# Summing gathered expert rows by 64x64 products on the four quarters of TensorE, one token tile after the other

## The chip, the cores and the metric

One core of one Trainium2 chip runs the whole program. The metric is the device time of one execution in microseconds (us); lower is better. The engines are TensorE (PE in the profile, its weight loads PEld), VectorE (DVE), ScalarE (ACT), GpSimd (POOL) and SyncE (SP). A float32 product is recorded as two MATMULs with a weight load each, so 16 records of a 128x512 product are 8 products.

## The reference

One step of a 2-layer decoder trunk, for 512 prompt tokens and 64 sample tokens. Each layer normalises x, runs three token mixers, merges and projects them back onto x, and then adds the output of a retrieval of single-neuron experts. That last part is where the change is:

```python
def _peer(h, w_query, subkeys, w_up, w_down):
    q = (xt @ w_query).reshape(n, PEER_HEADS, 2, PEER_DKEY // 2)        # 8 heads
    s = jnp.einsum('nhpd,pkd->nhpk', q, subkeys)
    s1, i1 = lax.top_k(s[:, :, 0], PEER_TOPK)                            # top 16
    s2, i2 = lax.top_k(s[:, :, 1], PEER_TOPK)
    cand = (s1[..., :, None] + s2[..., None, :]).reshape(n, PEER_HEADS, 256)
    best, ic = lax.top_k(cand, PEER_TOPK)
    expert = ...                                                         # i1 * 128 + i2
    gate = jax.nn.softmax(best, axis=-1)
    up = jnp.take(w_up, ek, axis=0)                                      # one row of 1024 a choice
    act = jax.nn.gelu(jnp.einsum('nd,nhkd->nhk', xk, up)) * gk
    down = jnp.take(w_down, ek, axis=0)
    return jnp.einsum('nhk,nhkd->nd', act, down)                         # added to x
```

All is float32. Every token has 8 x 16 = 128 choices, each with an up row and a down row of 1024 floats, from tables of 16384 rows.

## The kernel before

The 576 tokens lie in 5 tiles: four of 128 prompt tokens, tile 4 with the 64 sample tokens. The stage with the change is `score_expert_stage`, once in each layer. A **choice** is one gather for one tile: 128 rows (one for each partition) of 2048 floats, the up row and the down row side by side, 1.05 MB. Tile 4 puts two of its choices into one gather, so there are 4 x 128 + 64 = 576 gathers, worked through in 288 **groups** of two.

What a group goes through, engine by engine, each engine in the order in which its program is written:

- POOL (L2826) issues the gather into one of the places of a ring. It waits until the choice that last lay in that place has been summed (`downs_done`).
- DVE (L2868) multiplies the up row with the normalised token and sums the product, one instruction a choice. Between a group's dot products and its weights stands one quarter of the routing of a coming head, if the table `ROUTE_AT` has one for this group: the top-16 searches over scores (`Router.part`, L2404 to L2443), which give the ids that later gathers need.
- ACT (L2933) takes the gelu, DVE (L2880) multiplies it with the gates to `weight`, and ACT (L2944) makes a diagonal matrix of each choice's 128 weights.
- PE (L3036) multiplies the diagonal with the down row: two products of 128x128 by 128x512 a choice, added up in PSUM over all of a tile's choices. After the second the choice's place is free. x itself goes into the same sum by a product with the identity (`add_x`, L3002), so that at a tile's end ACT only copies PSUM back to x (`copy_x`, L2920).
- From the group `GATES_AT` on, one choice of two is not summed by PE: DVE adds weight times down row onto x or onto `own` (`BY_VECTOR`, `add_own`, L2857).

Also inside the stage: queries (L2966, eight products each, in a half of 256 or 128 columns and one of 320) and scores (L2995) for the later heads, which PE makes ahead of the sums of the group named in `asking`, and which ACT copies out (L2892, L2907) after that group's diagonals. Each query's weights (512 KB) come by SP into a ring of three. Tiles 0 and 1 are worked through together, head by head (`TOGETHER = 2`), the others one by one; so a head of routing lasts for 16 groups at first. In layer 0, the groups after `GATES_AT` carry products for the next layer as well (`following.tensor`, L1335 and L1330).

The ring of places (`place_of`): ten places for the first `BEGUN` = 90 choices, eight up to choice `EXTENDED` = 244, then ten again, two of them in room that is free once the last query is done. Before choice `FREE_FIRST` = 3, POOL waits for the end of the output projection.

Of the kernel before, what the change touches and what calls it, by code (L numbers as in the profile page):

```python
# [16 lines left out]
D = 1024  # L17
# [2450 lines left out]
TOGETHER = 2  # L2468
HEADS = [(n, h) for h in range(PH) for n in range(TOGETHER)] + [(n, h) for n in range(TOGETHER, TILES) for h in range(PH)]
BY_GROUP = [(n, h * TOPK + c) for n, h in HEADS[:(TILES - 1) * PH] for c in range(0, TOPK, GROUP)]  # L2470
BY_GROUP += [(TILES - 1, c) for c in range(0, COUNT[TILES - 1], GROUP)]
ROUTE_AT = {}
for _h in range(PH):
    _start = _h * TOGETHER * STEP
    _parts = {0: (1, _h), 8: (0, _h + 1), 12: (TOGETHER, _h)} if _h < PH - 1 else {0: (1, _h), 8: (TOGETHER, _h)}
    for _at, _head in _parts.items():
        ROUTE_AT.update({_start + _at + k: _head + (k,) for k in range(4)})
for _i, _head in enumerate(itertools.product(range(TOGETHER + 1, TILES), range(PH), range(4))):
    ROUTE_AT[TOGETHER * PH * STEP + _i] = _head
# [8 lines left out]
EXTENDED = 244  # L2488
Q_RING = 3
NEAR = 2 * P  # L2490
ASKED = ((0, 2), (3, 4), (6, 9), (11, 13))
FIRST_ASKED, REST_ASKED = ((3, 5), (5, 6), (8, 10), (12, 13)), (0, 2)

FREE_FIRST = 3
BEGIN, BEGUN = (8, 9, 7, 0, 1, 2, 3, 4, 5, 6), 90
# [21 lines left out]
ROUTES_DONE = max(max(ROUTE_AT), TILE_END[TOGETHER] + 5)  # L2517
BATCHES = ((0, 1, 2), ROUTES_DONE + 3), ((3,), TILE_END[TILES - 2] + 5)
# [45 lines left out]
BY_VECTOR = [q for q in range(2 * GATES_AT, PAIRS - 6) if q % 2 == 1]  # L2564
BY_TENSOR = [q for q in range(PAIRS) if q not in BY_VECTOR]
SUMMED = list(itertools.accumulate(0 if q in BY_VECTOR else 1 for q in range(PAIRS)))
TILE_OF = [n for n, c0 in BY_GROUP for k in range(GROUP)]
FIRST_SUM = min(q for q in BY_TENSOR if TILE_OF[q] == LAST_TILE - 1)
FIRST_OWN = min(q for q in BY_VECTOR if TILE_OF[q] == LAST_TILE)
added_by = lambda q: len([k for k in BY_VECTOR if k <= q])  # L2570


class NextNorm:
# [13 lines left out]
    def sync(self, sp):  # L2587
# [17 lines left out]
        else:  # L2605
# [3 lines left out]
            for i in range(2):  # L2609
                sp.wait_ge(s.added, len(BY_VECTOR))  # L2610
                sp.wait_ge(s.downs_done, SUMMED[PAIRS - 5 + 2 * i])
                to, src = self.places.first_slab(i)
                sp.dma_start(to, src).then_inc(s.in_slab[i], 16)

    def scalar(self, act, i):
# [3 lines left out]
        for n in squares_at(i):  # L2619
# [4 lines left out]
            act.wait_ge(s.x_copied, n + 1)  # L2624
# [71 lines left out]
    def last_scalar(self, act):  # L2696
# [5 lines left out]
        act.wait_ge(s.summed, TILES)  # L2702
        act.wait_ge(s.square_half, 1)
        for a in range(2):
            if a:
                act.wait_ge(s.x_half, 1)
                act.wait_ge(s.square_half, 2)
            nc.scalar.activation(self.junk[0:NS, 0:512], g.ps[0:NS, self.bank(a), :], ACT.Square, accum_out=self.spare[0:NS, a:a + 1]
                                 ).then_inc(s.square_half, 1)
# [7 lines left out]
    def bank(self, a):  # L2717
        return 2 * (LAST_TILE % 2) + a

    def last_vector(self, dve, link):  # L2720

        nc, g, s = self.nc, self.g, self.g.s
        dve.wait_ge(s.summed, TILES)
        for a in (1, 0):
            if a == 0:
                dve.wait_ge(s.square_half, 2)
            nc.vector.tensor_copy(g.x[0:NS, LAST_TILE, a * 512:(a + 1) * 512], g.ps[0:NS, self.bank(a), :]).then_inc(s.x_half, 1)
# [24 lines left out]
def score_expert_stage(nc, g, t, l, rows, sc, sc0, ids, gates, router, late, w_q, out, sb, following):  # L2752
# [7 lines left out]
    diag = sb("diag", [P, DIAGS, P])  # L2760
    mixed = g.space(AT_MIXED)("mixed", [P, MIXED, 2 * D])
    own = g.space(AT_MIX + KT * TOK + 2 * D + 16)("own", [P, D])
# [9 lines left out]
    halves = [(u + v, a) for u in range(0, NQ, 2) for a in range(2) for v in range(2)]  # L2772
    columns = lambda u, a: slice(NEAR, TOK) if a else slice(P if u < 2 else 0, NEAR)
    asked = lambda u, a: halves.index((u, a)) + 1
    asking = [[] for _ in BY_GROUP]
# [12 lines left out]
    with nc.Block() as block:  # L2788
# [41 lines left out]
        def _(dve):  # L2830
# [30 lines left out]
            for i, (n, c0) in enumerate(BY_GROUP):  # L2861
# [8 lines left out]
                if i:  # L2870
                    add_own(i - 1)
# [353 lines left out]
```

## Time and profile before

| | us |
|---|---|
| median of 3 runs | 5051.02 (5049.02 to 5064.87) |
| the profiled execution, its span | 5042.8 |
| layer 0: first gather to last dot product of the expert stage | about 1096 to 2683 |
| layer 1: the same | about 3530 to 5030 |

Over the span PE is busy 87%, PE's weight loads 51%, DVE 63%, ACT 24%, POOL 32%. A busy share of PE is not PE at its peak, since products are pipelined and overlap in the records. Gathers go through the queue that the profile calls software_dynamic; its packets took 61.4% of the span of the 16 DMA engines. The rows used for the forecast stand further down, each group with its view and columns.

### The profile page before, as it was taken

Reading aid. Unit: us, or ns where it says so; the run is one execution under the profiler, and the core shown is the slowest. Engines: PE = TensorE matmul, PEld = TensorE weight load, DVE = VectorE, ACT = ScalarE, POOL = GpSimd, SP = SyncE. Lnnn points to the kernel's source line nnn. Section 1 sums busy time; section 2 is a strip of 40 time slices with the busy share of each in tenths; the row PEclk is TensorE's granted clock in tenths of the full one; section 3 lists DMA queues with packets and bytes.
Section 4 is the critical chain, followed back from the end, with each engine's and each line's share of the span. In section 5 each row is a group of like instructions: output and inputs, shape, how many; then the busy total and the mean of one; then the engine's idle time right before and its main releaser. Section 6 shows DMA issues by size and latency. Waiting matters only on the chain. (4 is left out here: it accounts for less than half of the span.)

```text
span 5042.8 us, 49934 instructions
## 1 busy us (share of the span) xinstructions
PE 4367.6 (87%) x17024; PEld 2583.3 (51%) x17024; DVE 3163.9 (63%) x7441; ACT 1188.3 (24%) x2971; POOL 1621.6 (32%) x1418
## 2 busy tenths in 40 slices
PE   8899999999989877789999897799999987777555
PEld 6866677755444323334476776776544443232111
DVE  6523323247878789855556644432778788995776
ACT  2211211113323323221111223110333232332111
POOL 0412000014444444433330241100444444444554
PEclk9999999999999999999999999999999999999777
DMA  2223232329999999999993234441999999999998
GB/s 110 84 74 120 73 127 96 137 115 415 415 409 410 416 420 413 412 420 419 419 419 149 84 109 166 169 163 40 387 419 404 412 413 420 420 413 418 416 414 342
DMA packets 266368, 1472.42 MB, mean 292 GB/s; under 512 B 27009, under 2 KB 77953, under 8 KB 113601
## 3 DMA queue, kind: packets, MB, share of 16 engines
q0 software_dynamic: 176608, 1263.35, 61.4%
q1 hardware_dynamic: 79168, 198.75, 10.7%
q10 hardware_dynamic: 10336, 7.12, 0.5%
q8 instruction: 135, 2.21, 0.2%
q14 instruction: 121, 0.98, 0.1%
HBM read 1433.90 MB, written 55.34 MB: 295 GB/s over the span
## 5 line engine op out<-in xcount | busy, mean ns | idle before, releaser
L3036 PE MATMUL ps<-early,diag 128*128 128x512 f32 (+1 forms) x3464 | 1692.2, 634 | 416.8 <-ACT diag L2944 416.3
L2826 POOL DMA_INDIRECT early<-in_peer,ids x980 | 1148.4, 1172 | 1430.1 <-PE ps L3036 1257.6
L2868 DVE SCALAR_TENSOR_TENSOR early<-early,rows 128x1024 f32<-128x1024 f32 x980 | 1184.2, 1223 | 443.9 <-DMA early<-in_peer,ids 441.8
L3036 PEld LDWEIGHTS ps<-early,diag 128*128 128x128 f32 (+1 forms) x3464 | 647.8, 195 | 1370.6 <-ACT diag L2944 679.0
L2944 ACT ACTIVATE diag<-consts_sb,weight 128x128 f32<-128x128 f32 (+1 forms) x1010 | 354.3, 391 | 769.5 <-DVE weight L2880 754.0
L1335 PE MATMUL ps<-hT,gate_ring 128*128 128x288 f32 (+2 forms) x1728 | 465.0, 424 | 6.4 <-ACT gate_out L1347 3.4
L1335 PEld LDWEIGHTS ps<-hT,gate_ring 128*128 128x128 f32 x1728 | 319.7, 193 | 144.9 <-issue 34.6
L2933 ACT ACTIVATE gel<-dot 128x2 f32<-128x2 f32 x576 | 117.4, 204 | 1116.3 <-DVE early L2868 925.0
L3036 PE MATMUL ps<-late,diag 128*128 128x512 f32 (+1 forms) x432 | 228.5, 671 | 83.5 <-ACT diag L2944 82.7
L2966 PE MATMUL ps<-late 128*128 128x320 f32 (+2 forms) x1024 | 251.8, 399 | 0.0
L2826 POOL DMA_INDIRECT late<-in_peer,ids x136 | 164.6, 1211 | 199.2 <-PE ps L3036 163.5
L2966 PEld LDWEIGHTS ps<-late 128*128 128x128 f32 x1024 | 189.7, 190 | 74.5 <-issue 28.9
L2868 DVE SCALAR_TENSOR_TENSOR late<-late,rows 128x1024 f32<-128x1024 f32 x136 | 165.1, 1224 | 85.0 <-DMA late<-in_peer,ids 84.8
L2826 POOL DMA_INDIRECT mixed<-in_peer,ids x36 | 43.1, 1198 | 503.5 <-DVE ids L2443 438.2
L3036 PEld LDWEIGHTS ps<-late,diag 128*128 128x128 f32 (+1 forms) x432 | 81.3, 200 | 223.6 <-ACT diag L2944 133.8
L1314 POOL DMA_DIRECT2D gate_rows<-gate_out x48 | 26.4, 549 | 455.1 <-ACT gate_out L1347 412.1
L426 PE MATMUL ps<-hT,ring 128*128 128x288 f32 x512 | 168.5, 411 | 2.4 <-PEq L2788 1.1
L427 PE MATMUL ps<-hT,ring 128*128 128x288 f32 x512 | 167.0, 408 | 0.0
L2880 DVE TENSOR_TENSOR weight<-gel,gates 128x2 f32<-128x2 f32 x576 | 92.2, 160 | 101.5 <-ACT gel L2933 95.1
L1347 ACT COPY gate_out<-ps 128x384 f32<-128x384 f32 (+2 forms) x126 | 52.7, 418 | 380.6 <-PE ps L1335 342.9
L2345 DVE TENSOR_TENSOR term<-slot,ps 128x288 f32<-128x288 f32 x32 | 14.5, 454 | 178.8 <-PE ps L2284 178.8
L2283 PE MATMUL ps<-oc,slot 128*128 128x288 f32 x384 | 124.5, 406 | 0.0
(394 smaller groups left out, 5859.3 us busy)
## 6 DMA issues: line engine op xcount, KB each, us to landing
gate_ring<-in_in_gate POOLq DMA_DIRECT2D x48, 512.0 KB, 4.2
slot<-in_w_branch SPq DMA_DIRECT2D x16, 1152.0 KB, 5.2
ring<-in_in_delta SPq DMA_DIRECT2D x8, 2048.0 KB, 8.4
late<-in_peer_query SPq DMA_DIRECT2D x32, 512.0 KB, 7.9
early<-in_peer,ids POOLq DMA_INDIRECT x980, 15.5
slot<-gate_rows SPq DMA_DIRECT2D x16, 864.0 KB, 7.0
slot<-in_in_pool SPq DMA_DIRECT2D x6, 2048.0 KB, 10.7
gate_ring<-in_in_gate SPq DMA_DIRECT2D x24, 512.0 KB, 10.8
```

The lines of the kernel that those rows point to most:

```text
L426: nc.tensor.matmul(part_a(g, u), weights(k), rhs(k)[:, 0:HALF], start=k == 0, stop=k == nk - 1)
L427: last = nc.tensor.matmul(part_b(g, u), weights(k), rhs(k)[:, HALF:TOK], start=k == 0, stop=k == nk - 1)
L1335: last = nc.tensor.matmul(g.ps[:, bank, 0:c.stop - c.start], self.ring[:, i % GATE_RING, k, :], hT[:, k, c], start=k == 0, stop=k == KT - 1)
L1347: self.nc.scalar.copy(self.out[:, i % GATE_OUT, at:at + c.stop - c.start], g.ps[:, bank, 0:c.stop - c.start]).then_inc(s.gate_copied, 1)
L2283: nc.tensor.matmul(g.ps[:, u % 2, 0:HALF], w, self.src[b][:, k, 0:HALF], start=k == 0, stop=k == nk - 1)
L2826: pool.indirect_dma_start(place(q), None, table_rows, bass.IndirectOffsetOnAxis(ap=ids[:, n, c:c + 1], axis=0)).then_inc(s.pair[PLACE[q]], 16)
L2868: nc.vector.scalar_tensor_tensor(out=up, in0=up, scalar=1.0, in1=rows[:, n, :], op0=ALU.mult, op1=ALU.mult, accum_out=dot[:, i % 2, k:k + ...
L2880: nc.vector.tensor_tensor(weight[:, i % 2], gel[:, i % 2], gates[:, n, c0:c0 + GROUP], ALU.mult).then_inc(s.weighted, 1)
L2933: nc.scalar.activation(gel[:, i % 2], dot[:, i % 2], ACT.Gelu).then_inc(s.gelus, 1)
L2944: nc.scalar.activation(diag[:, d % DIAGS, 0:ROWS[n]], table(g, "ident" if ROWS[n] == P else "ident2"), ACT.Copy, scale=weight[:, i % 2, k: ...
L2966: last = nc.tensor.matmul(g.ps[:, 4 + i % 2, 0:c.stop - c.start], late.ring[:, u % Q_RING, k, :], late.hT[:, k, c], start=k == 0, stop=k = ...
L3036: ins = nc.tensor.matmul(g.ps[0:r, 2 * (n % 2) + m, :], diag[:, (SUMMED[q] - 1) % DIAGS, 0:r], place(q)[:, D + m * 512:D + (m + 1) * 512], ...
```

## The change

The down rows are summed in another shape. A tile's 128 tokens are cut into two halves of 64 (r = 0, 1), and the diagonal is only 64 columns wide (`diag` [P, DIAGS, NS], made from `ident2`). A product is 64x64 by 64x512: half r of choice k (k = 0, 1 of the group) is multiplied on the rows r and the columns k of the array, and lands in PSUM partitions 64k to 64k+63 of bank 2r + m. A group has eight such products instead of four. `downs_done` rises once a group, after the last product, instead of once a choice.

Since a tile takes all four banks, and both choices have sums of their own, DVE adds the two to x at a tile's end (`fold`: four additions of 64x1024), after the first group of the next tile has had its dot products; PE waits for that before the next tile's first sum. `add_x`, `copy_x`, `BY_VECTOR` and `own` are gone. At the stage's end DVE adds the sample tile's two sums to x, in halves of 512 columns (`last_vector`).

Tiles now go strictly in turn, so a head of tile 0 lasts 8 groups, and routing has all of the first 160 groups but four. Queries and scores move forward: those of heads 0 and 1 stand ahead of the first sum or in the first three groups (`FIRST_ASKED`, `REST_ASKED`), the others end in group 47. The ring has ten places up to choice 32, eight up to choice 114, then ten. `GATES_AT` moves from group 214 to 209.

```diff
-TOGETHER = 2
-HEADS = [(n, h) for h in range(PH) for n in range(TOGETHER)] + [(n, h) for n in range(TOGETHER, TILES) for h in range(PH)]
+HEADS = [(n, h) for n in range(TILES) for h in range(PH)]
...
-EXTENDED = 244
+EXTENDED = 114
...
-BEGIN, BEGUN = (8, 9, 7, 0, 1, 2, 3, 4, 5, 6), 90
+BEGIN, BEGUN = (8, 9, 7, 0, 1, 2, 3, 4, 5, 6), 32
...
-                    if LAST[q] in BY_VECTOR:
-                        pool.wait_ge(s.added, added_by(LAST[q]))
-                    elif LAST[q] >= 0:
-                        pool.wait_ge(s.downs_done, SUMMED[LAST[q]])
+                    if LAST[q] >= 0:
+                        pool.wait_ge(s.downs_done, LAST[q] // GROUP + 1)
...
+            def fold(n):
+                dve.wait_ge(s.downs_done, TILE_END[n] + 1)
+                for r in range(2):
+                    rows_of_half = slice(r * NS, (r + 1) * NS)
+                    to = g.x[rows_of_half, n, :].rearrange("p (a c) -> p a c", a=2)
+                    link(nc.vector.tensor_tensor(to, to, g.ps[0:NS, 2 * r:2 * r + 2, :], ALU.add))
+                    nc.vector.tensor_tensor(to, to, g.ps[NS:P, 2 * r:2 * r + 2, :], ALU.add).then_inc(s.x_copied, 1)
...
+            def sums(i, n, m):
+                for r, k in ORDER_OF_TILES:
+                    q, half = i * GROUP + k, slice(r * NS, (r + 1) * NS)
+                    last = nc.tensor.matmul(g.ps[k * NS:(k + 1) * NS, 2 * r + m, :], diag[half, q % DIAGS, :],
+                                            place(q)[half, D + m * 512:D + (m + 1) * 512], start=i == tile_group(n), stop=i == TILE_END[n])
+                return last
...
             for i, (n, c0) in enumerate(BY_GROUP):
...
+                pe.wait_ge(s.diagonal, (i + 1) * GROUP)
+                for m in range(2):
+                    last = sums(i, n, m) if n < LAST_TILE else sample_sums(i, n, m)
+                last.then_inc(s.downs_done, 1)
```

The order on PE at the start of the stage in a layer, before: L2966 is a query, L2995 scores, L3002 `add_x`, L3036 the sums; mixed and early are places of the ring.

```order
1101 L2995 MATMUL ps<-late_5895,qT_5909 128x128 x2
1102 L3002 MATMUL ps<-x,consts_sb 128x512 x2
1103 L2966 MATMUL ps<-late_5895 128x320 x8
1104 L3036 MATMUL ps<-mixed_5914,diag_5913 128x512 x4
1105 L3036 MATMUL ps<-early_5908,diag_5913 128x512 x4
1106 L2966 MATMUL ps<-late_5895 128x320 x8
```

The same place after the change (L2937 is a query, L2966 scores, L2981 the sums):

```order
1101 L2966 MATMUL ps<-late_5895,qT_5909 128x128 x2
1102 L2937 MATMUL ps<-late_5895 128x320 x8
1103 L2937 MATMUL ps<-late_5895 128x256 x8
1104 L2966 MATMUL ps<-late_5895,qT_5909 128x128 x2
1105 L2966 MATMUL ps<-late_5895,qT_5909 64x128
1106 L2937 MATMUL ps<-late_5895 128x320 x8
1107 L2937 MATMUL ps<-late_5895 128x256 x8
1108 L2966 MATMUL ps<-late_5895,qT_5909 128x128 x2
1109 L2966 MATMUL ps<-late_5895,qT_5909 64x128
1110 L2966 MATMUL ps<-late_5895,qT_5909 128x128 x4
1111 L2937 MATMUL ps<-late_5895 128x320 x8
1112 L2937 MATMUL ps<-late_5895 128x256 x8
1113 L2981 MATMUL ps<-mixed_5914,diag_5913 64x512 x8
```

Between the first scores and the first sum stood one query; now six stand there, with the scores of four.

The first gathers on POOL after the change; before it, the rows up to here read the same (with L2826), but `downs_done` was counted by choice:

```order
152:150 L2810 DMA early_5908<-in_peer,ids_5880 128x2048 [waits out_sum]
153:151 L2810 DMA early_5908<-in_peer,ids_5880 128x2048 x6
154:152 L2810 DMA mixed_5914<-in_peer,ids_5880 128x2048 [waits downs_done] x2
155:153 L2810 DMA early_5908<-in_peer,ids_5880 128x2048 [waits downs_done] x4
```

Ten gathers are issued without a sum; the eleventh waits for the first group's sums.

## Rows read from the trace of the kernel before

**Rows 1.** The page: span, DMA busy tenths and rate in 40 slices

```profile
span 5042.8 us, 49934 instructions
...
DMA  2223232329999999999993234441999999999998
GB/s 110 84 74 120 73 127 96 137 115 415 415 409 410 416 420 413 412 420 419 419 419 149 84 109 166 169 163 40 387 419 404 412 413 420 420 413 418 416 414 342
```

**Rows 2.** Windows: start:end, length, busy us of PE, PEld, DVE, ACT, POOL, PEclk, DMA share, GB/s

```profile
3542.00:3634.00 92.00, 89.84 (x302) 51.12 (x300) 69.68 (x194) 31.09 (x87) 45.42 (x37) 1.00 0.98 396
3634.00:3799.00 165.00, 152.19 (x424) 78.18 (x424) 135.60 (x384) 51.68 (x144) 71.33 (x63) 0.98 1.01 418
3799.00:4199.00 400.00, 356.92 (x952) 176.84 (x952) 324.74 (x906) 123.75 (x339) 173.09 (x155) 0.97 1.00 410
4199.00:4450.00 251.00, 194.48 (x401) 75.37 (x400) 227.56 (x672) 76.88 (x194) 116.32 (x100) 0.96 1.01 419
4450.00:5011.00 561.00, 364.36 (x612) 118.38 (x611) 407.91 (x795) 102.59 (x296) 295.78 (x219) 0.83 1.01 415
```

**Rows 3.** Windows, the same columns: layer 0 from group 208 on

```profile
2191.00:2662.00 471.00, 443.60 (x1738) 259.99 (x1737) 281.24 (x457) 76.47 (x219) 170.08 (x151) 0.98 1.02 419
```

**Rows 4.** Chain of waits in order of time (start, us, what), at the start of layer 1

```profile
3561.73 4.31 PE ps L2966 x16
...
3570.47 3.45 PE ps L2966 x16
3573.92 3.43 PE ps L3036 x8
```

**Rows 5.** Timeline (start, us, engine, line, operation, shapes): products on parts of the array

```profile
3469.67 8.78 PE L2294 MATMUL ps<-w_out,merged 128*64 128x512 f32 x32 [1.95 <-DVEq L2352]
3478.38 7.13 PE L2300 MATMUL ps<-w_out,merged 128*128 128x512 f32 x16
...
3060.39 1.00 PE L1593 MATMUL ps<-qkT 64*128 64x128 f32 x12 [1.07 <-PEq L1420]
...
3199.37 1.30 PE L1826 MATMUL ps<-vc,pT 128*32 128x128 f32 x40
```

**Rows 6.** Window, L2294 alone: length, busy us of PE and PEld, PEclk, DMA share, GB/s

```profile
3471.50:3472.50 1.00, 1.00 (x5) 0.33 (x3) 0.50 1.00 340
```

**Rows 7.** Timeline: from the first ten gathers to the eleventh, layer 1

```profile
3542.76 0.94 POOL L2826 DMA_INDIRECT early<-in_peer,ids  x1 [8.77 <-PE ps L2300]
...
3550.39 4.47 PE L2966 MATMUL ps<-late 128*128 128x320 f32 x16
...
3551.72 0.94 POOL L2826 DMA_INDIRECT early<-in_peer,ids  x1 [0.30 <-issue]
...
3554.70 3.60 PE L3036 MATMUL ps<-mixed,diag 128*128 128x512 f32 x8
...
3556.85 0.94 POOL L2826 DMA_INDIRECT mixed<-in_peer,ids  x1 [4.18 <-PE ps L3036]
```

**Rows 8.** Windows of 4 us at the same place (columns as rows 2)

```profile
3548.00:3552.00 4.00, 3.62 (x12) 2.23 (x13) 3.59 (x12) 3.36 (x7) 3.09 (x4) 1.00 0.93 340
3552.00:3556.00 4.00, 4.00 (x15) 2.48 (x14) 3.86 (x12) 1.59 (x6) 0.67 (x1) 1.00 1.01 424
```

**Rows 9.** L2826 from 3850 to 4050 us: issue to landing

```profile
DMA to landing us min/median/max: 7.4/11.1/15.9
```

**Rows 10.** Window with a routing quarter in every group (columns as rows 2)

```profile
4284.00:4410.00 126.00, 96.59 (x199) 37.23 (x198) 117.33 (x350) 39.49 (x98) 58.91 (x50) 0.96 1.01 420
```

**Rows 11.** Waits of DVE in the same stretch: total, times, longest

```profile
DVE early L2868 <- DMA early<-in_peer,ids: 2.3, 4, 0.7
DVE late L2868 <- DMA late<-in_peer,ids: 0.7, 1, 0.7
```

**Rows 12.** Timeline: an addition from PSUM, and the stage's end in layer 1

```profile
3542.53 0.69 DVE L2363 TENSOR_TENSOR x<-x,ps 128x512 f32<-128x512 f32 x1 [5.58 <-PE ps L2300]
...
5034.47 1.88 PE L3049 MATMUL ps<-own,consts_sb 128*64 128x512 f32 x4
...
5037.16 0.59 ACT L2708 ACTIVATE junk<-ps 64x512 f32<-64x512 f32 x1
```

More of the change, by code:

```diff
@@ L2561, in gates_at @@
     return [v for v in range(GATE_RUNS[RUN_AHEAD].total) if GATES_AT + 4 * v // 3 == i]
[L2564 to L2570, printed above, removed]
+ORDER_OF_TILES = ((0, 0), (1, 1), (0, 1), (1, 0))
 class NextNorm:
@@ L2771, in score_expert_stage @@
     slots = ROUTE_AT
[L2772 removed]
+    asking = [asked_at(i) for i in range(len(BY_GROUP))]
+    halves = [(u, a) for part in [FIRST_ASKED] + asking for kind, u, a in part if kind == "query"]
     columns = lambda u, a: slice(NEAR, TOK) if a else slice(P if u < 2 else 0, NEAR)
     asked = lambda u, a: halves.index((u, a)) + 1
[L2775 to L2786 removed]
+    tile_group = lambda n: min(i for i, (m, c) in enumerate(BY_GROUP) if m == n)
     with nc.Block() as block:
@@ L2997, in scores, with ask, sample_sums @@
                 last.then_inc(s.far_sums if a else s.pe_b, 1)
-            def add_x(n, first):
-                r = ROWS[n]
-                for m in range(2):
-                    last = nc.tensor.matmul(g.ps[0:r, 2 * (n % 2) + m, :], ident(g, r), g.x[0:r, n, m * 512:(m + 1) * 512],
-                                            start=first, stop=not first)
+            def ask(kind, u, a):
+                if kind == "query":
+                    query(u, a)
+                else:
+                    scores(u, a)
+            def sums(i, n, m):
[4 more added lines that the diff above has]
+                return last
+            def sample_sums(i, n, m):
+                for k in range(GROUP):
+                    q = i * GROUP + k
+                    last = nc.tensor.matmul(g.ps[k * NS:(k + 1) * NS, m, :], diag[:, q % DIAGS, :],
+                                            place(q)[:, D + m * 512:D + (m + 1) * 512], start=i == tile_group(n), stop=i == TILE_END[n])
                 return last
@@ L3018, in _ @@
             for i, (n, c0) in enumerate(BY_GROUP):
[L3019 to L3023 removed]
+                if c0 == 0 and n:
+                    pe.wait_ge(s.x_copied, 2 * n)
                 for kind, u, a in asking[i]:
[L3025 to L3028 removed]
+                    ask(kind, u, a)
@@ L3029, in _ @@
                 following.tensor(pe, i)
-                for k in range(GROUP):
-                    q = i * GROUP + k
-                    if q in BY_VECTOR:
-                        continue
-                    pe.wait_ge(s.diagonal, SUMMED[q])
-                    for m in range(2):
-                        ins = nc.tensor.matmul(g.ps[0:r, 2 * (n % 2) + m, :], diag[:, (SUMMED[q] - 1) % DIAGS, 0:r],
-                                               place(q)[:, D + m * 512:D + (m + 1) * 512], start=q == FIRST_SUM,
-                                               stop=n < LAST_TILE - 1 and c0 + k == COUNT[n] - 1)
-                    ins.then_inc(s.downs_done, 1)
@@ L3040, in _ @@
-                if i == TILE_END[n] and n < LAST_TILE - 1:
-                    pe.wait_ge(s.downs_done, SUMMED[(i + 1) * GROUP - 1])
-                    pe.sem_inc(s.summed, 1)
-                if i == TILE_END[LAST_TILE - 1] + 1:
-                    pe.wait_ge(s.added, added_by(TILE_END[LAST_TILE - 1] * GROUP + 1))
-                    add_x(LAST_TILE - 1, False).then_inc(s.summed, 1)
-                if i == TILE_END[LAST_TILE]:
-                    pe.wait_ge(s.added, len(BY_VECTOR))
-                    for m in range(2):
-                        last = nc.tensor.matmul(g.ps[0:r, 2 * (n % 2) + m, :], table(g, "ident2"), own[:, m * 512:(m + 1) * 512],
-                                                start=False, stop=True)
-                    last.then_inc(s.summed, 1)
+                pe.wait_ge(s.diagonal, (i + 1) * GROUP)
```

147 lines of the change are left out of this document (54 added, 93 removed).

## Prediction

> **What bounds the kernel now.** I read the page first: the rate of the DMA engines in 40 slices. In two stretches, slices 10 to 21 and 29 to 40, it stands at 409 to 420 GB/s with a busy share of nine tenths or more, and elsewhere at 40 to 170 [rows 1]. These two stretches are the two expert stages, and the change touches nothing outside them. Then the windows by ring size: in layer 1 the share of the DMA engines is 1.00 or 1.01 from 3634 to 5011 us, at 410 to 419 GB/s, though PE is busy there for anything from 65% to 92% of the time and DVE for 73% to 91% [rows 2]. Layer 0 is the same down to its last groups, where PE is busiest: 419 GB/s [rows 3]. So what ends last in an expert stage is the transfer of the gathers. A group moves 2 x 128 x 8192 bytes = 2.10 MB, which at 415 GB/s takes 5.05 us. A layer moves 288 of them, some 1456 us, and the change moves exactly the same bytes.
>
> What PE has to do in a group: a record of 512 columns takes 3.43 / 8 = 0.429 us, a group of four products (eight records) 3.43 us [rows 4]. That is below 5.05 us. A query costs 4.31 us for 320 columns and 3.45 us for 256 [rows 4], 15.5 us for a head's four, some 17.7 us with its scores (20 records of 128 columns, 0.107 us each by columns). Over 16 groups: 16 x 3.43 + 17.7 = 73 us against 16 x 5.05 us of gathers plus 1.05 MB of query weights (2.5 us), 83 us. PE has room before.
>
> **Part 1: the sums on quarters.** Does the array do four of these at once? A 64x64 tiling with float32 does not occur in the trace; its two halves do. Products of 64 columns (128*64) put alternately on both halves of the columns: 32 records of 512 columns take 8.78 us and full products 7.13 us for 16 [rows 5], and that although the first microseconds of the 32 ran at a granted clock of 0.50 [rows 6]. Some 8 records at 0.43 us and 24 at 0.215 us make 8.6 us: at the full clock two records cost what one does. Products on alternate halves of the rows (64*128, 128 columns): 12 records in 1.00 us, of which the last lasts 0.29, leaves 0.065 us from start to start, where 128 columns take 0.107 us [rows 5]. And four column tiles of 32: 40 records in 1.30 us, 0.026 us from start to start, a quarter of 0.107 [rows 5]. So I take four at once: 16 records of 0.429 us in 4 x 0.429 = 1.72 us, and half of the 3.43 us is gone. The bound on the other side is 16 x 0.429 = 6.9 us with no overlap, or 3.43 us if only two overlap.
>
> A rule of the Trainium skill speaks against this part. The row: after the last 128*64 record the first 128*128 one starts with the next timeline row, 3478.38, while 32 records from 3469.67 end at 3478.45 and a record lasts 0.59, so the last one started near 3477.86: a step of 0.5 us where 0.43 is usual between full products [rows 5]. The Trainium skill, "TensorEngine Tiling (Array Packing)", section "Key Properties", says that a change of the tiling mode drains TensorE. By the row that is at most 0.3 us a change; with two changes a group PE's 1.72 us would become 2.3 us, and the sum below stays as it is, because PE has still 2.7 us to spare.
>
> What this buys on the path: nothing while DMA is the bound. It brings a release of places a little forward: before, a group's two choices came free 1.7 and 3.4 us after the first diagonal was ready, now both after the second diagonal (0.35 us later) and 1.7 us: on the mean 0.5 us earlier in a cycle of 20 to 25 us. I count it at nothing (bounds: -2 to 0 us a layer).
>
> **Part 2: tiles in turn, and the start.** This is where I expect the change to show. Ten gathers can be under way before any sum; the eleventh waits for the first group's sums. Before, the last of the ten is issued at 3551.7, the first sums start at 3554.7 with one query ahead of them, and the eleventh gather leaves at 3556.85 [rows 7], while the DMA engines still have work. After, PE does the following from 3548.7 on (that query's start at 3550.39 less the 1.7 us of `add_x`): queries of 4.31, 3.45, 4.31 and 3.45 us with the scores of four, then (`REST_ASKED` and group 0's own) 4.31 and 3.45 us. That is 23.3 us of queries [rows 4], 2.2 us of scores and about 2 us for hand-overs with ACT: group 0's sums start near 3576.3 and end near 3578.3 (1.72 us and 0.27 us of latency). The eleventh gather leaves at 3578.6 instead of 3556.85.
>
> When do the DMA engines run dry? From 3542.8 on they have seven gathers (7.34 MB) and about three query loads (1.57 MB), 8.9 MB. Up to 3552 they move at most 340 GB/s, 2.9 MB in all, and then 424 GB/s [rows 8]: the other 6.0 MB last for 14.2 us, to about 3566.5. So they stand idle for 12 us. Group 1 is next: ahead of its sums stand a score, and queries of 4.31 and 3.45 us, so it ends at 3578.3 + 10.4 = 3588.7, whereas the two gathers issued at 3578.6 and 3579.9 are done by 3584: 5 us more. Two query loads fall into these holes and give back 2 x 1.25 us. From group 2 on the releases (3591.8, 3597, 3603.6, ...) are ahead of the transfers. Until about group 16 only two to four gathers are under way, and by the first window, 396 GB/s against 418 in the next [rows 2], a short queue costs some rate: 2 us more. Sum: 12 + 5 - 2.5 + 2 = 16.5, I take **+17 us a layer**. Bounds: +8, if the loads and the shortest landings (7.4 us [rows 9]) fill more of the holes, and +25, if PE, ACT and DVE, which now wait for each other in turn (gelu of a group stands behind the copies of the query before it), need until group 16 to get going.
>
> **Part 3: the ring.** With ten places 418 and 419 GB/s (the two windows around), with eight 410 GB/s [rows 2]. Eight places hold for 154 choices before and 82 after. 36 groups of 5.2 us, 187 us, at 1.9% more: **-3.5 us a layer**. Later windows with ten places show 415 [rows 2], hence bounds of -5 and -1.
>
> **Part 4: routing in all groups.** Groups 0 to 159 now have a quarter each. Before, groups 128 to 191 had that: DVE busy for 117.3 of 126 us, waiting for DMA for 3.0 us [rows 10, 11], at 420 GB/s. So DVE needs 123 us for the 25 groups, 4.92 us a group, against 5.05 us of transfer, and in the first 48 groups 5.37 us (with query weights). It fits, barely. It holds for PE too: 8 x 1.72 + 17.7 = 31.5 us in 8 groups of 43 us.
>
> **Part 5: fold.** An addition of 128x512 from PSUM takes 0.69 us [rows 12], one of 1024 columns some 1.25 us, four of them 5 us and 0.6 us of waiting for PE. DVE is late by that at groups 64, 128, 192 and 256. The ring covers it: landed gathers wait, fewer are under way, about as few as with eight places, and DVE wins back 0.13 us a group, so 40 groups at half of 1.9% lose 2 us. Two of the four lie in the dense part; at the others DVE has slack. **+3 us a layer** (0 to +8). BY_VECTOR's additions go (in groups where DVE had slack): nothing.
>
> **Part 6: the end.** The last sums take 1.72 instead of 3.43 us and the product with `own` (L3049, 1.7 us) goes, but DVE adds four times 0.69 us before the last square of ACT, where before square and copy ran together, 1.5 us [rows 12]: 3.4 us less, 2.4 us more, **-1 us a layer** (-3 to +2, if PE runs at the lower clock there).
>
> **Sum.** 17 - 3.5 + 3 - 1 = 15.5 us a layer, 31 us for both; the span goes from 5042.8 to 5074 us. The profiled execution lies 8.2 us below the median of the runs shown, which I keep: 5051 + 31 = **5082 us**. In layer 0 the same rows and waits recur, and the products for the next layer after group 209 find the same 419 GB/s.
>
> **The rivals.**
> - *No difference that a measurement can tell* (within 0.3%, 15 us): the holes at the start are filled to half (+8 a layer), the rest cancels: about 5058 us. For it: 61% of the DMA time is gathers whatever PE does. Against it: the ten places are a count, and ten is reached by 3552.
> - *Faster*: a shorter queue is the reason for the 410 and 415 GB/s, and with PE's part of a place's cycle halved and ten places early the rate is 418 from group 16 on: 400 us at 2% and 561 us at 0.7% are 12 us a layer. With +3 at the start and -1 at the end: -10 us a layer, 5031 us. Against it: the windows with the least PE work have 415, not the most [rows 2].
> - *DVE becomes the bound*: with the copies of a head's four queries in eight groups, not sixteen, a group needs 5.5 us instead of 5.37 for the first 48, and 5.15 instead of 5.05 for groups 48 to 159: 6 + 11 us a layer on top of the 15.5, 5116 us. It decides as soon as waits add 0.13 us to the 4.92 us.
> - *The quarters don't work at once*. With pairs only, PE needs 3.43 + 0.5 us a group: 49 us for 8 groups with queries against 43, 36 us a layer, and in layer 0 after group 209 3.9 us + 2.9 us against 6.3: 36 us more; 5190 us. With none, 6.9 us a group bound both stages: over 6000 us. The Trainium skill, "TensorE: Matmul & The Clock Gate", Part 3, has a 4x4 packing run 10.6 times as fast; by it this rival is out, and the rows on halves agree as far as they go.
>
> **How the numbers follow.** Chances: forecast 0.48, DVE the bound 0.13, quarters not at once 0.07 (slower in all: 0.68); within 0.3% 0.20; faster 0.12. The likeliest's own range is 5066 to 5105 (its bounds: +8 to +27 a layer). For 8 in 10 the range reaches down over most of the no-difference case and up over the DVE case: 5045 to 5120. A measurement of this kernel tells about 0.3% from no change.
>
> **What would show it.** Right: in the changed profile the eleventh gather of a layer leaves some 20 us later than before against its first, with the DMA share near zero in two holes behind it; the sums' 16 records take near 2 us; the windows from group 16 on stay at 410 to 419 GB/s; the additions of fold take 1.2 us each. Wrong: an eleventh gather that isn't late; a rate above 420; DVE waiting for nothing in the first 160 groups while the rate falls below 405; 16 records in 3.4 us or more.

## The result, and the profile after

The changed kernel takes 5093.62 us (median of 4 runs, 5085.61 to 5099.81) against 5051.12 us for the kernel before beside it: a ratio of 1.0083, 95% interval 1.0065 to 1.0102. It is slower, by about 42 us; 31 us were forecast. The kernel before has two usual times about 11 us apart, some 5047 and some 5058 us, so its median moves a little from comparison to comparison, and it is the ratios that count.

The page of the changed kernel, to be read against [rows 1]; PEclk is the granted TensorE clock in tenths:

```profile
span 5098.0 us, 59052 instructions
...
PEclk9999999999977677799998999899997777777777
DMA  2223242329999999999993234441899999999998
GB/s 109 84 83 115 71 144 86 118 111 393 398 418 417 419 394 419 420 419 419 414 418 138 83 124 148 172 163 42 336 401 403 419 419 392 419 420 420 420 416 354
```

Apart from their edge slices the two expert stages still stand at nine tenths or more. Their first slice is lower, 393 against 415 and 336 against 387 GB/s; later slices at 392 to 403 are made up for by others at 419 and 420. From the first dot product of a stage to its last (starts of L2868 before, L2845 after), layer 0 takes 1589.6 us against 1567.6, layer 1 1502.7 against 1480.8: 22 us more in each. The spans differ by 55 us. The other 12 lie between the stages, 878.5 us against 866.5, and belong to no part of the change: the variants of either kernel below show 870 to 879 there.

Where in the stage? I cut it at the first dot product of group 16. Windows of the changed kernel (columns as [rows 2]), layer 1:

```profile
3581.70:3689.00 107.30, 98.84 (x538) 58.78 (x538) 77.17 (x230) 36.01 (x107) 38.79 (x33) 0.98 0.84 339
3689.00:5084.30 1395.30, 830.39 (x4440) 234.96 (x4440) 1039.00 (x2680) 338.12 (x1020) 609.79 (x538) 0.78 1.00 411
```

And of the kernel before, cut at the same groups:

```profile
3548.10:3634.30 86.20, 84.45 (x258) 46.36 (x258) 67.08 (x193) 28.74 (x82) 41.05 (x34) 1.00 1.00 410
3634.30:5028.90 1394.60, 1080.39 (x2405) 452.02 (x2406) 1106.34 (x2773) 357.02 (x979) 657.70 (x536) 0.91 1.00 412
```

The whole loss is in the first 16 groups: 107.3 us against 86.2. The 272 groups after them take 1395.3 against 1394.6 us at the same mean rate, although PE is busy for 250 us less. Layer 0 reads the same: 107.0 against 86.2, then 1482.6 against 1481.4. The 272 groups are equal only in sum: groups 16 to 47 take 5.50 us each instead of 5.15 (397 against 418 GB/s), 11 us in all, and the groups after them win it back.

The first 16 groups cut once more, at group 8. After:

```profile
3581.70:3647.50 65.80, 62.63 (x326) 40.09 (x326) 38.78 (x116) 21.17 (x63) 20.32 (x17) 1.00 0.74 289
3647.50:3689.00 41.50, 36.21 (x212) 18.69 (x212) 38.38 (x117) 14.84 (x44) 18.47 (x17) 0.96 1.01 418
```

And before:

```profile
3548.10:3590.20 42.10, 41.83 (x140) 25.07 (x141) 28.91 (x78) 15.69 (x45) 18.21 (x16) 1.00 1.01 414
3590.20:3634.30 44.10, 42.63 (x119) 21.29 (x117) 38.17 (x116) 13.05 (x37) 22.84 (x19) 1.00 1.00 406
```

Groups 0 to 7 take 65.8 us instead of 42.1, with PE busy for 62.6 of them and the DMA engines for three quarters. Groups 8 to 15 are 2.6 us faster than before: there the DMA engines are full at 418 GB/s, and PE has room.

The start of the changed kernel on its timeline (L2937 a query, L2966 scores, L2981 the sums), to be read against [rows 7]:

```profile
3582.23 7.93 PE L2937 MATMUL ps<-late 128*128 128x320 f32 x32
...
3590.89 4.57 PE L2937 MATMUL ps<-late 128*128 128x320 f32 x16
3595.80 3.72 PE L2937 MATMUL ps<-late 128*128 128x256 f32 x16 [0.33 <-DMA late<-in_peer_query]
...
3602.06 7.92 PE L2937 MATMUL ps<-late 128*128 128x320 f32 x32
3609.91 1.95 PE L2981 MATMUL ps<-mixed,diag 64*64 64x512 f32 x16
```

On POOL, the eleventh gather, which waited 25.94 us for those sums:

```profile
3612.16 1.68 POOL L2810 DMA_INDIRECT mixed<-in_peer,ids  x1 [25.94 <-PE ps L2981]
```

And the DMA engines around it, in windows of 4 us (the last two numbers are share and GB/s):

```profile
3604.00:3608.00 4.00, 4.00 (x18) 3.11 (x17) 3.60 (x11) 1.22 (x4) 0.00 (x0) 1.00 0.11 38
3608.00:3612.00 4.00, 4.00 (x27) 2.12 (x26) 1.85 (x7) 1.06 (x4) 0.00 (x0) 1.00 0.29 93
3612.00:3616.00 4.00, 4.00 (x18) 2.84 (x18) 3.79 (x12) 0.53 (x2) 2.63 (x2) 1.00 0.36 80
3616.00:3620.00 4.00, 4.00 (x19) 3.28 (x18) 0.09 (x1) 0.42 (x1) 0.00 (x0) 1.00 1.00 412
3620.00:3624.00 4.00, 4.00 (x29) 1.97 (x28) 2.60 (x7) 1.32 (x5) 1.00 (x1) 1.00 0.44 170
```

These are the two holes of the forecast, and PE is busy for all of every window. The share of 0.84 over 107.3 us means 17 us of idle DMA engines; from 3628 us on, 46 us after the first dot product, every window of 4 us up to group 16 has a share of 0.99 or more. The 16 records of the sums take 1.95 us where eight full ones took 3.60 [rows 7]: four quarters do work at once.

### The profile page after: what moved, and what is told of

It is laid out like the page before. It is cut to its first block and busy times, and to the rows that moved or that the text cites. A ratio compares the mean times of both kernels' runs of the same rounds, so it can differ in the third digit from the quotient of the medians.

```text
span 5098.0 us, 59052 instructions
## 1 busy us (share of the span) xinstructions
PE 3922.8 (77%) x21640; PEld 2181.3 (43%) x21640; DVE 3045.2 (60%) x7335; ACT 1163.3 (23%) x3105; POOL 1584.7 (31%) x1418
## 5 line engine op out<-in xcount | busy, mean ns | idle before, releaser
L2981 PE MATMUL ps<-early,diag 64*64 64x512 f32 x6784 | 1109.3, 783 | 732.0 <-ACT diag L2921 732.0
L2810 POOL DMA_INDIRECT early<-in_peer,ids x948 | 1084.6, 1144 | 1422.3 <-PE ps L2981 1118.3
L2845 DVE SCALAR_TENSOR_TENSOR early<-early,rows 128x1024 f32<-128x1024 f32 x948 | 1140.1, 1222 | 455.1 <-DMA early<-in_peer,ids 448.6
L2981 PEld LDWEIGHTS ps<-early,diag 64*64 64x64 f32 x6784 | 264.5, 161 | 1503.8 <-ACT diag L2921 1092.8
L2921 ACT ACTIVATE diag<-consts_sb,weight 128x64 f32<-128x64 f32 x1152 | 338.0, 340 | 686.4 <-DVE weight L2857 666.2
L2981 PE MATMUL ps<-late,diag 64*64 64x512 f32 x1280 | 220.1, 818 | 173.8 <-ACT diag L2921 173.3
L2810 POOL DMA_INDIRECT late<-in_peer,ids x188 | 215.2, 1145 | 286.6 <-PE ps L2981 214.4
L2845 DVE SCALAR_TENSOR_TENSOR late<-late,rows 128x1024 f32<-128x1024 f32 x188 | 226.6, 1222 | 115.6 <-DMA late<-in_peer,ids 115.6
L2937 PE MATMUL ps<-late 128*128 128x320 f32 (+2 forms) x1024 | 262.4, 412 | 0.3 <-DMA late<-in_peer_query 0.3
L2937 PEld LDWEIGHTS ps<-late 128*128 128x128 f32 x1024 | 189.9, 194 | 94.0 <-issue 47.2
L2981 PEld LDWEIGHTS ps<-late,diag 64*64 64x64 f32 x1280 | 51.4, 165 | 334.8 <-ACT diag L2921 247.7
L2990 PE MATMUL ps<-early,diag 128*64 128x512 f32 x400 | 125.3, 761 | 71.6 <-ACT diag L2921 71.6
```

What stands on the lines that cost most here:

```text
L2810: pool.indirect_dma_start(place(q), None, table_rows, bass.IndirectOffsetOnAxis(ap=ids[:, n, c:c + 1], axis=0)).then_inc(s.pair[PLACE[q]], 16)
L2845: nc.vector.scalar_tensor_tensor(out=up, in0=up, scalar=1.0, in1=rows[:, n, :], op0=ALU.mult, op1=ALU.mult, accum_out=dot[:, i % 2, k:k + ...
L2921: nc.scalar.activation(diag[:, q % DIAGS, :], table(g, "ident2"), ACT.Copy, scale=weight[:, i % 2, k:k + 1]).then_inc(s.diagonal, 1)
L2937: last = nc.tensor.matmul(g.ps[:, 4 + i % 2, 0:c.stop - c.start], late.ring[:, u % Q_RING, k, :], late.hT[:, k, c], start=k == 0, stop=k = ...
L2981: last = nc.tensor.matmul(g.ps[k * NS:(k + 1) * NS, 2 * r + m, :], diag[half, q % DIAGS, :], place(q)[half, D + m * 512:D + (m + 1) * 512] ...
L2990: last = nc.tensor.matmul(g.ps[k * NS:(k + 1) * NS, m, :], diag[:, q % DIAGS, :], place(q)[:, D + m * 512:D + (m + 1) * 512], start=i == t ...
```

## The experiments

**Is the start the cause? The queries first, in the kernel before.** Ten queries and scores move ahead of group 0's sums; all else stays.

```diff
+    ahead = [("query", 0, 1), ("query", 1, 1), ("scores", 0, 1), ("scores", 1, 1), ("query", 2, 0), ("query", 3, 0), ("scores", 2, 0),
+             ("scores", 3, 0), ("query", 2, 1), ("query", 3, 1)]
+    for listed in asking:
+        listed[:] = [asked_for for asked_for in listed if asked_for not in ahead]
+    asking[0][:] = ahead
```

> The kernel before with one thing of the change: the first ten queries and scores stand ahead of group 0's sums (19.7 us more of queries there, taken from the groups up to 13); sums, order of tiles and ring as before. Theory 1 (start): the eleventh gather leaves some 21 us later, the DMA engines idle for about 12 us in each layer, about 5051 + 24 = 5075 us. Theory 2 (something else in the change): 5051 us.

Measured: 5078.95 us, ratio 1.0046 (1.0028 to 1.0064), about 23 us. The stages take 15.6 and 14.5 us longer, 12.3 and 12.5 of them in the first 16 groups; the eleventh gather leaves 33 us after the first dot product instead of 8.7. So queries ahead of the first sums cost time by themselves, without quarters, fold or tiles in turn.

**Does a leaner start of the changed kernel get it back?** Only the queries that group 0's routing needs stay ahead; the others follow the sums of group 0 or stand in groups 2 to 8.

```diff
-FIRST_ASKED = (... six queries, six scores)
+FIRST_ASKED = (("query", 0, 0), ("query", 1, 0), ("scores", 0, 0), ("scores", 1, 0), ("query", 2, 0), ("scores", 2, 0), ("query", 0, 1))
...
-                for kind, u, a in asking[i]:
+                for kind, u, a in asking[i] if i else ():
...
+                for kind, u, a in asking[i] if i == 0 else ():
+                    ask(kind, u, a)
```

> The changed kernel with fewer queries ahead of the first sums: only the near half of unit 2 with its scores and the far half of unit 0 (7.8 us of queries instead of 23.3); the others are spread over groups 0 to 8, those of group 0 behind its sums. Theory 1 (the loss is the start: the eleventh gather waits for the first sums and the DMA engines run dry): the eleventh gather leaves about 11 us after the first dot product instead of 30, one hole of some 4 us is left, some 6 us a layer over the kernel before: about 5064 us. Theory 2 (the loss comes from routing in all groups, fold or the lower TensorE clock): stays at 5093 us.

Measured: 5099.66 us, ratio 1.0088 (1.007 to 1.0106). A miss. The eleventh gather leaves 15 us after the first dot product as meant, and the first 16 groups take 110.8 us in layer 1, more than the 107.3 of the changed kernel. DVE's and POOL's waits in this run, layer 1, 3581 to 3640 us (total, times, longest):

```profile
POOL early L2811 <- PE ps L2982: 26.7, 4, 14.3
POOL mixed L2811 <- PE ps L2982: 14.1, 2, 10.3
DVE top L2404 <- ACT sc L2892: 13.2, 2, 10.8
```

DVE now stands 10.8 us for the scores that were put later, the dot products queued behind that wait stand too, and the hole opens after group 1 (no DMA traffic at all from 3608 to 3612).

**Can the order be mended?** Two more orders. In the first, routing is one group later and every group's queries stand behind its sums (the new lists of queries are left out of both cuts):

```diff
-        ROUTE_AT.update({_h * STEP + _at + k: _head + (k,) for k in range(4)})
+        ROUTE_AT.update({_h * STEP + _at + k + 1: _head + (k,) for k in range(4)})
...
-                for kind, u, a in asking[i]:
+                for kind, u, a in ():
...
+                for kind, u, a in asking[i]:
+                    ask(kind, u, a)
```

> The changed kernel with a start without either wait: ahead of the first sums only the far half of unit 0 and the near half of unit 2 with its scores; each group's queries stand behind its sums; unit 3's near half comes right after group 0's sums; and all routing quarters of the first 64 groups start one group later, so that group 0 routes nothing. In the run before, with only the queries moved, the eleventh gather left early, but DVE stood 10.8 us in group 1 for the scores of unit 3, and groups 0 to 7 still took 8.0 us each. Theory 1 (the loss of the change is its start: sums and routing of the first groups wait for the queries and the query weights of head 1): groups 0 to 7 take 6 us or less each, the loss of a layer against the kernel before falls from 22 to about 7 us: about 5065 us. Theory 2 (any order of tiles in turn loses it elsewhere): stays above 5085 us.

Measured: 5325.13 us, ratio 1.0543 (1.052 to 1.0565): 7.9 to 9.7 us a group up to group 47. ACT copies a query ahead of the next gelu, so a query behind the sums is waited for in full. Timeline of layer 0, one such round (L2984 sums, L2940 query, L2872 its copy, L2916 gelu):

```profile
1302.77 1.95 PE L2984 MATMUL ps<-early,diag 64*64 64x512 f32 x16 [2.90 <-ACT diag L2924]
...
1304.65 4.57 PE L2940 MATMUL ps<-late 128*128 128x320 f32 x16
...
1309.26 0.42 ACT L2872 COPY qT<-ps 128x320 f32<-128x320 f32 x1 [6.54 <-PE ps L2940]
1309.58 0.21 ACT L2916 ACTIVATE gel<-dot 128x2 f32<-128x2 f32 x1
...
1310.71 1.95 PE L2984 MATMUL ps<-early,diag 64*64 64x512 f32 x16 [1.49 <-ACT diag L2924]
```

The second has the later routing too, few queries ahead, two groups with queries behind the sums, and all others ahead of them:

```diff
-                for kind, u, a in asking[i]:
+                for kind, u, a in asking[i] if i >= 2 else ():
...
+                for kind, u, a in asking[i] if i < 2 else ():
+                    ask(kind, u, a)
```

> The start of the last variant (first sums after the far half of unit 0 and the near half of unit 2; routing one group later), but with a group's queries ahead of its sums again from group 2 on, and head 2's queries spread to group 9. With them behind the sums, groups 8 to 47 took 8 us each: PE's query, ACT's copy of it, and the next gelu, weight, diagonal and sums all came one after the other. Theory 1 (the loss is the start): groups 0 to 7 take 6.2 us or less, groups 8 to 47 5.4 to 5.6 as in the changed kernel, some 8 us a layer less loss than 22: about 5065 to 5070 us. Theory 2 (the work of heads 0 to 2 has to be done in the first 8 groups in whatever order, so the same time is lost behind another wait): groups 0 to 7 take 7 us or more, 5085 us or more.

Measured: 5088.86 us, ratio 1.0068 (1.0045 to 1.009). The longest wait of POOL falls from 25.9 to 12.0 us, and the first 16 groups still take 106.4 us; the small gain lies in groups 16 to 47. The changed kernel and two of these orders need 106 to 111 us for the first 16 groups. What an order wins in groups 0 to 7 (63.9 us with the leaner start and 59.4 in the last one, against 65.8) it loses in groups 8 to 15 (46.8 and 47.3 against 41.5). So the order decides where the time is lost; none of those tried gets rid of it.

**What sets them.** The row that I had passed over is PE's busy time: 98.8 of 107.3 us after, 84.5 of 86.2 before, 100.2 of 106.4 (the last order) and 100.6 of 110.8 (the leaner start). It is really work, not pipelined waiting: a query alone takes 3.7 to 4.6 us in the timeline. PE's part by line in the first 16 groups of layer 1, after (length, busy PE and PEld, PEclk, DMA share, GB/s): queries, scores, sums.

```profile
3581.70:3689.00 107.30, 57.91 (x224) 41.66 (x224) 0.98 0.84 339
3581.70:3689.00 107.30, 12.95 (x74) 9.29 (x74) 0.98 0.84 339
3581.70:3689.00 107.30, 30.59 (x240) 8.00 (x240) 0.98 0.84 339
```

And before, in the same order:

```profile
3548.10:3634.30 86.20, 25.11 (x96) 18.16 (x96) 1.00 1.00 410
3548.10:3634.30 86.20, 5.56 (x34) 4.68 (x34) 1.00 1.00 410
3548.10:3634.30 86.20, 53.57 (x120) 22.31 (x120) 1.00 1.00 410
```

A query has 16 records: 14 queries stand in these groups instead of six. They and the scores cost 40 us more, the quarters give 23 us back, and the 3.8 us of `add_x` are gone. Ten of the 14 queries stand in groups 0 to 7: 41.3 us of queries, 9.4 us of scores and 13.6 us of sums there, in a stretch that took 42.1 us before. Any order that keeps all this work in the first 16 groups needs at least its 98.8 us, 12.6 us more than the 86.2 us of before. To test it from both sides, PE's work was taken away in the changed kernel (each query sums four of its eight products, so other experts are picked) and added in the kernel before.

```diff
-                for k in range(KT):
+                for k in range(KT // 2):
...
-                                            late.hT[:, k, c], start=k == 0, stop=k == KT - 1)
+                                            late.hT[:, k, c], start=k == 0, stop=k == KT // 2 - 1)
```

> The changed kernel, but each query sums four of its eight products (the other half of the sum is left out, so the routing picks other experts; every copy, score, routing step, gather and wait stays). In the changed kernel's first 16 groups of layer 1 TensorE is busy for 98.8 of 107.3 us: 57.9 us are 14 queries, 13 are scores, 31 are sums; before, six queries took 25.1 us, and TensorE was busy for 84.5 of 86.2 us. Theory 1: TensorE's work sets the pace of these groups, whatever its order; without 29 us of it, the transfers do, about 40 MB at 415 GB/s or 92 to 95 us: 12 to 15 us a layer less, 5066 to 5072. Theory 2: the chain of hand-overs (query, ACT's copy, scores, routing, gelu, diagonal) sets it, and the products are the smaller part: first 16 groups above 102 us, 5083 or more.

Measured: 5063.17 us, ratio 1.0025 (1.0011 to 1.0038). In the kernel before:

```diff
-                for k in range(KT):
+                for k in list(range(KT)) * (2 if 2 <= i < 8 else 1):
```

> The kernel before, but the six queries of the first 16 groups of each layer are computed twice in place, the second time over the first: 24 to 25 us more of TensorE's work a layer in these groups, nothing else. Theory 1 (TensorE's work sets the pace at the start, with the ring's ten places as the only cover): 15 to 24 us a layer more, 5085 to 5105, first 16 groups 101 us or more. Theory 2 (the chain of hand-overs or the transfers set it, TensorE's busy share of 98% being pipelined waiting): up to 8 us a layer, under 5073.

Measured: 5094.75 us, ratio 1.0089 (1.0073 to 1.0106). The first 16 groups of layer 1, halved queries in the first row, doubled ones in the second (columns as [rows 2]):

```profile
3559.90:3655.70 95.80, 75.03 (x426) 39.08 (x426) 76.79 (x228) 36.17 (x108) 40.84 (x34) 0.95 0.94 374
3568.80:3679.10 110.30, 108.57 (x354) 64.64 (x354) 67.31 (x193) 28.60 (x81) 41.39 (x34) 1.00 0.83 321
```

Doubling added 24.1 us of queries (49.25 instead of 25.11 us) and the groups became 24.1 us longer: one for one. Halving took 25.6 us of queries away (32.27 left) and gave 11.5 us, by when DMA is back at a share of 0.94; nearly all of it lies in groups 0 to 7 (54.9 us instead of 65.8). Groups 16 to 47 also gain, 5.37 us each instead of 5.50. Theory 1 holds in both, and the second is the cleaner one: the kernel before has its PE and its DMA at their limits together in these groups, so every microsecond given to PE there counts. In the changed kernel PE's work sets the time in groups 0 to 7, and the transfers in groups 8 to 15. How its 21 us divide between the order, which alone cost 12.5 us in the kernel before, and the added work, no run separates.

**Are the quarters worth anything?** The changed kernel with full products again, into two banks, each added to x at the tile's end:

```diff
-    diag = sb("diag", [P, DIAGS, NS])
+    diag = sb("diag", [P, DIAGS, P])
...
-                for r, k in ORDER_OF_TILES:
-                    q, half = i * GROUP + k, slice(r * NS, (r + 1) * NS)
-                    last = nc.tensor.matmul(g.ps[k * NS:(k + 1) * NS, 2 * r + m, :], diag[half, q % DIAGS, :],
+                for k in range(GROUP):
+                    q = i * GROUP + k
+                    last = nc.tensor.matmul(g.ps[:, m, :], diag[:, q % DIAGS, :], place(q)[:, D + m * 512:D + (m + 1) * 512],
```

> The changed kernel with the prompt tiles' sums as full 128x128 products again (four a group, two banks; fold is two additions of 128x512); order, ring and queries as changed. Theory 1: PE then needs 8 x 3.43 + 17.7 = 45.2 us and hand-overs for 8 groups with queries against 43 to 44 us of transfers, and the first two groups' sums come 1.7 us later each; 10 to 15 us a layer more than the changed kernel: 5113 to 5123 us. Theory 2 (DMA hides PE everywhere): 5093 us.

Measured: 5180.79 us, ratio 1.0248 (1.0229 to 1.0268), far more than expected. In each layer the first 48 groups take about 18 us longer than in the changed kernel, 10 in the first 16 and 8 in the next 32. In layer 0 groups 208 to 255, which carry the products for the next layer, take 7.17 us each instead of 6.24, 45 us together. Windows of this kernel in the first 16 groups of layer 1, and inside groups 208 to 255 of layer 0 (columns as [rows 2], the second to be read against [rows 3]):

```profile
3646.90:3764.10 117.20, 115.99 (x410) 72.87 (x411) 77.05 (x230) 37.78 (x107) 32.40 (x32) 1.00 0.82 322
```

```profile
2235.00:2740.00 505.00, 500.39 (x2034) 295.06 (x2034) 183.59 (x374) 87.95 (x279) 164.04 (x145) 1.00 0.96 377
```

PE bounds both. At the start it is busy for 116.0 of 117.2 us; the quarters take 22 us of sums away there and 10 us of the time. In the later window it is busy for 500 of 505 us, and the rate falls to 377 GB/s. `BY_VECTOR` had taken half of the sums off PE in those groups, and it is gone; the quarters replace it.

**Does the order of the quarters matter?** Both column halves of one quarter in a row, so that neighbours in the program go to the same part of the array:

```diff
+                if m == 0:
+                    return None
                 for r, k in ORDER_OF_TILES:
...
+                    for b in range(2):
+                        last = nc.tensor.matmul(g.ps[k * NS:(k + 1) * NS, 2 * r + b, :], diag[half, q % DIAGS, :],
...
```

> The changed kernel with the prompt tiles' eight products of a group in another order: both halves of the columns of one quarter in a row, then the next quarter. Theory 1 (the quarters work at once whatever the order, since the following products wait only for their own quarter): 16 records within 2.4 us, the time unchanged at about 5093 us. Theory 2 (products are taken strictly in order, one that waits for its quarter holds all behind it): about 3 us, and since PE's room in layer 0 after group 209 gets small, up to 5120 us.

Measured: 5097.59 us (two runs), ratio 1.0088 (1.0061 to 1.0114). The group of the sums on its page, beside the changed kernel's:

```profile
L2982 PE MATMUL ps<-early,diag 64*64 64x512 f32 x6784 | 1109.4, 777 | 720.0 <-ACT diag L2921 716.8
```

```profile
L2981 PE MATMUL ps<-early,diag 64*64 64x512 f32 x6784 | 1109.3, 783 | 732.0 <-ACT diag L2921 732.0
```

The same busy time, to 0.1 us.

**Fold.** The four additions cut to 16 columns, so that most of a tile's sums are left out of x:

```diff
-                    to = g.x[rows_of_half, n, :].rearrange("p (a c) -> p a c", a=2)
+                    to = g.x[rows_of_half, n, :].rearrange("p (a c) -> p a c", a=2)[:, :, 0:8]
...
+                    link(nc.vector.tensor_tensor(to, to, g.ps[0:NS, 2 * r:2 * r + 2, 0:8], ALU.add))
...
```

> The changed kernel with the additions of fold cut from 1024 columns to 16 (8 in each of two banks), so the prompt tiles' sums are left out of x but for those columns; everything waits as before. Theory 1 (the ring covers fold but for 3 us a layer): about 5087 us. Theory 2 (DVE bounds the first 160 groups, every us on it counts): four times 5 us in a layer, about 5055 us. Theory 3 (fold is free): 5093 us.

Measured: 5089.4 us, ratio 1.0068 (1.005 to 1.0086). Its stages take 1590.0 and 1499.3 us, 0.4 more and 3.4 less than with fold. Fold costs 0 to 3 us a layer, and the intervals of the two ratios overlap, so a cost above nothing isn't shown.

**The ring.** The kernel before with eight places from choice 30 on instead of 90:

```diff
-BEGIN, BEGUN = (8, 9, 7, 0, 1, 2, 3, 4, 5, 6), 90
+BEGIN, BEGUN = (8, 9, 7, 0, 1, 2, 3, 4, 5, 6), 30
```

> The kernel before with eight places in the ring from choice 30 on instead of 90 (ten again from 244 on, as before). Theory 1 (eight places cost 1.9% of the rate against ten): 30 groups of 5.2 us, 3 us a layer, about +6 us. Theory 2 (the lower rate there comes from the query weights and routing in those groups, not from the ring): no change.

Measured: 5059.59 us, ratio 1.0014 (1.0003 to 1.0026), some 7 us (the medians of this comparison are only 2.4 us apart). The stages take 4.6 and 1.6 us longer. In groups 16 to 31 of layer 1 a group takes 5.23 us instead of 5.03. Eight places cost rate, about 4% there, but in groups 32 to 44, which also have eight now, no loss shows (5.24 against 5.20 us, and 5.17 against 5.19 in layer 0).

## Why the prediction was right, and where it was off

- **What bounds the kernel**: right for the stage from group 16 on as a whole: 1395.3 against 1394.6 us. Groups 16 to 47 were to take 5.37 us and take 5.50; with halved queries they take 5.37, so PE's work still counts a little there. Wrong for the start. I wrote "PE has room before" from 73 us of work against 83 us of transfer; the window of exactly these groups shows 84.5 us of PE in 86.2 us. My estimate had one head's four queries and 17.7 us for them where six stand, with 30.7 us of queries and scores. For the changed kernel I never summed PE's work of the first eight groups, which is 62.6 us; Part 4 has 31.5 us in 43 for eight later groups, where groups 8 to 15 show 36.2 in 41.5.
- **Part 1** (quarters work at once, nothing on the path): four at once is right, 1.95 us with the end of the pipeline against a forecast of 1.72. The drain that the Trainium skill names for a change of tiling mode ("TensorEngine Tiling (Array Packing)", "Key Properties") isn't visible beyond the 0.23 us between the two, and the run with another order of the quarters changed nothing. "Nothing on the path" failed twice: at the start the quarters take 22 us of sums off PE and are worth 10 us of time (and 8 more up to group 47), and from group 209 on in layer 0 they stand in for `BY_VECTOR`. With full products the changed kernel is slower by another 87 us by the medians.
- **Part 2** (+17 us a layer, bounds +8 to +25): right in size and in mechanism. The two holes came, and the eleventh gather leaves 30.5 us after the first dot product instead of 8.7 (+21.8 us, as worked out). The gathers released by groups 2, 3 and 4 leave 44.8, 49.2 and 55.1 us after it, where 43.7, 48.9 and 55.5 were worked out. The DMA engines are idle for 17 us; 12 and 5 less 2.5 were forecast. "From group 2 on the releases ... are ahead of the transfers" came true: the gathers released by group 2 leave at 3626.5, and from 3628 on the DMA engines are full. The price is 21.1 us in layer 1 and 20.8 in layer 0, 4 us over the forecast. An estimated 2.5 us of that are bytes: 107.3 us at 339 GB/s are 1 MB more than 86.2 us at 410. What this part doesn't say, and the experiments add, is that none of three other orders got rid of the hole: PE has 62.6 us of work in groups 0 to 7, a leaner start moved the loss into the next eight, and only less work for PE gained more than 1 us in the first 16. In the kernel before, where the work is smaller, the order alone costs 12.5 us a layer in these groups.
- **Part 3** (-3.5 us for the ring) and **Part 5** (+3 for fold): each agrees in size with its experiment, the ring 2 to 5 us a layer by the stages for 30 groups, fold 0 to 3 us a layer. In the changed kernel itself groups 57 to 127, nearly all with ten places instead of eight, take 361.2 us in layer 1 against 367.4, and groups 16 to 47, with eight instead of ten in most of them and with the queries moved forward, lose 11 us. The total of 1395.3 us is the sum of these and was not taken apart further. The additions of fold take 1.20 to 1.22 us each, as said.
- **Part 4** (routing in all groups fits barely): right. Groups 80 to 127 take 5.05 us in layer 1, and the rival with DVE as the bound fell. Groups 16 to 47 do take the 5.5 us that it names, but with halved queries and the same work for DVE (154 us in these groups in both) they take 5.37, so DVE doesn't set them.
- **Part 6** (-1 us a layer): from the last dot product to the end of the span 13.7 us, before 13.9.
- **The sum**: 31 us forecast, 44 us in the profiles' stages and 42 by the medians. The missing 13 are Part 2's 4 us a layer, and in each layer 2 us for the rest: -1.5 by Parts 3, 5 and 6, +0.7 and +1.2 in the rows after group 16, with the end at -0.2. The rivals *no difference*, *faster* and *quarters not at once* fell; the first assumed holes half filled, the second a rate of 418 GB/s from group 16 on, which is 411.

No version here beats the kernel before, and little is left to win by this route: its layer 1 stage takes 1480.8 us, of which 1394.6 run at 412 GB/s, and 250 us less work for PE there gained nothing.

## What to carry to other kernels

A resource with room on the average can be full in the first eight groups of a stage, where lookahead work for later steps is piled up: cut the window there and add up the busy time by line before calling an engine free. To tell an order from an amount of work, double the work in place; the answer here was one for one, where three new orders moved the wait or made it longer. A saving on an engine is worth what that engine holds up, stage by stage: against full products the quarters were worth 10 us in the first 16 groups, 8 in the next 32, 0 to 3 from there to group 207, and 45 us beside the next layer's products.

## What the runs showed of the hardware

- Four float32 64x64 products on the four quarters of the array, each with its own 512 columns of moving data, run at once: 16 records in 1.95 us against 3.60 us for eight full ones, in both orders of the program that were tried.
- The granted clock fell as TensorE had less to do: its mean over the last 272 groups of layer 1 is 0.78 with PE busy for 830 of 1395 us, against 0.91 before with 1080 us, and 0.94 in the changed kernel with full products, also 1080 us. The time of these groups is the same after as before, 1395 us, with the DMA engines at a share of 1.00, so no cost of the lower clock shows.
